# A conformer's depthwise convolution: one of eight feature tiles moves from TensorE to GpSimd

## The reference, cut to what matters

```python
def conformer_conv_mixer(x, w_pw1, b_pw1, w_dw, b_dw, ln_g, ln_b, w_pw2, b_pw2):
    h = x @ w_pw1 + b_pw1
    a, gate = jnp.split(h, 2, axis=-1)
    h = a * jax.nn.sigmoid(gate)
    h = causal_depthwise_conv(h, w_dw) + b_dw          # 31 taps, each feature by itself
    hf = h.astype(F32)
    mean = jnp.mean(hf, axis=-1, keepdims=True)
    var = jnp.mean(jnp.square(hf - mean), axis=-1, keepdims=True)
    hf = (hf - mean) * lax.rsqrt(var + LN_EPS) * ln_g.astype(F32) + ln_b.astype(F32)
    h = jax.nn.silu(hf).astype(x.dtype)
    return h @ w_pw2 + b_pw2
```

## Time and profile before

| what | value |
|---|---|
| median of the runs | 1980.66 us |
| the profiled execution's own time | 1981.02 us |
| its span in the profile | 1979.2 us |
| PE busy | 1964.8 us (99%) |
| DVE busy | 1342.4 us (68%) |
| ACT busy | 965.2 us (49%) |
| POOL busy | 46.2 us (2%), 89 instructions |

### The profile page before, as it was taken

The page is one execution under the profiler, slowest core; times in us unless marked ns, Lnnn a source line. Parts: engine busy times, 40 slices in busy tenths (PEclk is TensorE's granted clock), DMA queues, the critical chain, the costliest instruction groups (busy, mean ns, idle before and its releaser), DMA issues.

```text
span 1979.2 us, 26437 instructions
## 1 busy us (share of the span) xinstructions
PE 1964.8 (99%) x11074; PEld 1676.9 (85%) x11074; DVE 1342.4 (68%) x1496; ACT 965.2 (49%) x1148; POOL 46.2 (2%) x89
## 2 busy tenths in 40 slices
PE   9999999999999999999999999999999999999998
PEld 7889888888988887788888688889888888778887
DVE  5876666687566775676568866666865667667565
ACT  6655444655544543354445554454544444345443
POOL 0000000000000000000000000000000000000000
PEclk9999999999999999999999999999999999999999
DMA  8425654523665555546657455547565555455653
GB/s 256 131 86 172 205 190 158 172 97 124 220 202 187 190 172 190 171 146 195 209 194 207 130 197 189 191 154 234 192 202 191 172 195 187 159 173 170 200 191 107
DMA packets 239559, 351.70 MB, mean 178 GB/s; under 512 B 15952, under 2 KB 134096, under 8 KB 239440
## 3 DMA queue, kind: packets, MB, share of 16 engines
q1 hardware_dynamic: 238320, 348.22, 54.0%
q10 hardware_dynamic: 1120, 1.78, 0.3%
HBM read 344.83 MB, written 1.05 MB: 175 GB/s over the span
## 4 chain that ended last, share of the span: by engine, by line
PE 96%; DVE 2%; ACT 1%; DMA 1%; issue 1%; SPq 0%; DVEq 0%; ACTq 0%
PE psD L2205 19%; PE psD L2223 15%; PE psD L2224 15%; PE psD L2228 13%; PE psD L2214 9%; PE psD L2188 3%; PE psD L2187 3%; PE psD L2192 3%; PE psD L2226 2%; PE psD L2563 1%; PE psD L2511 1%; PE psD L2635 1%; PE psD L2636 1%; PE psD L2879 1%; PE psD L2307 1%; PE psD L2264 1%
## 5 line engine op out<-in xcount | busy, mean ns | idle before, releaser
L1217 DVE TENSOR_TENSOR wl<-raw,wh 128x2048 fp32r<-128x2048 f32 (+2 forms) x327 | 723.4, 2219 | 258.0 <-ACT wh L671 257.5
L671 ACT ACTIVATE wh<-raw 128x2048 fp32r<-128x2048 f32 (+2 forms) x327 | 605.3, 1855 | 303.2 <-PE psD L2226 243.0
L2205 PE MATMUL psD<-AHL,wh 128*128 128x512 f32 x1664 | 396.0, 390 | 0.0
L2205 PEld LDWEIGHTS psD<-AHL,wh 128*128 128x128 f32 x1664 | 307.8, 188 | 60.9
L2223 PE MATMUL psD<-wh,HH 128*128 128x512 f32 x864 | 339.1, 392 | 0.1
L2224 PE MATMUL psD<-wl,HH 128*128 128x512 f32 x864 | 336.6, 390 | 0.0
L2228 PE MATMUL psD<-wh,HL 128*128 128x512 f32 x735 | 286.1, 389 | 0.0
L2214 PEld LDWEIGHTS psD<-AHL,wl 128*128 128x128 f32 x1560 | 200.9, 191 | 8.1
L2214 PE MATMUL psD<-AHL,wl 128*128 128x256 f32 x1560 | 203.4, 283 | 0.0
L2223 PE MATMUL psD<-wh,AHL 128*128 128x512 f32 (+3 forms) x504 | 194.5, 386 | 1.7 <-DVE AHL L1253 1.7
L2223 PEld LDWEIGHTS psD<-wh,HH 128*128 128x128 f32 x864 | 162.4, 188 | 33.4 <-DVE wl L1217 0.5
(11 more groups left out here) (407 smaller groups left out, 2277.5 us busy)
## 6 DMA issues: line engine op xcount, KB each, us to landing
raw<-in_mlp_w SPq DMA_DIRECT2D x128, 1024.0 KB, 5.4
raw<-in_ret_w_in SPq DMA_DIRECT2D x48, 1024.0 KB, 5.2
raw<-in_w_gate SPq DMA_DIRECT2D x20, 1024.0 KB, 5.4
raw<-in_w_up SPq DMA_DIRECT2D x20, 1024.0 KB, 5.3
raw<-in_w_down SPq DMA_DIRECT2D x20, 1024.0 KB, 5.6
raw<-in_ret_w_out SPq DMA_DIRECT2D x16, 1024.0 KB, 5.0
raw<-in_w_in SPq DMA_DIRECT2D x15, 1024.0 KB, 5.5
raw<-in_cf_w_pw SPq DMA_DIRECT2D x12, 1024.0 KB, 6.1
```

Source lines behind the costliest of these rows:

```text
L671: e.activation(wh[q % NHL][:, 0:kt * n], raw[q % NRAW][:, 0:kt * n], ACT.Copy).then_inc(*up("act_wh", q))
L1217: e.tensor_tensor(wl[q % NHL][:, 0:kt * n], raw[q % NRAW][:, 0:kt * n], wh[q % NHL][:, 0:kt * n].bitcast(F32), ALU.subtract).then_inc(*up( ...
L2205: e.matmul(psD[pair][:, f, :], hi[:, k, fs], both[:, k, :, :], start=k == 0, stop=False, skip_group_check=True)
```

## The change

Feature 3 leaves PE's list: `CONV` has six entries. GpSimd takes it in 62 instructions. It waits for `hp` 3, then makes for each of the 31 taps a product (a tensor_scalar), and adds it to one of two partial sums (a tensor_tensor), even and odd taps apart; the first product of each starts its sum. One addition joins the two in `HC` feature 3 (after PE's first feature, whose tap weights lay there), and one multiplication makes its square. The four buffers of this are `PT3`, whose place is free because PE's copies of features 0 to 3 shrink to 0 to 2. Every addition waits for its product, every product for the addition before last.

DVE builds one set of tap weights less, does `taps` in steps to 14, 22, 28 and 31 in place of 8, 18, 26 and 31, and adds GpSimd's feature and square last (`pool_sums`), in place of the fifth `sums`. PE waits for these two additions before it sums `SM` and `SS`. The tap weights and PSUM banks of the features behind feature 3 move up by one place, and so features 4, 5 and 6 are PE's fourth, fifth and sixth.

```diff
-CONV = (0, 1, 2, 3, 4, 5, 6)
-TAPS = {"a": (0, 4), "b": (4, 2), "c": (6, 1)}
-CBANK = (0, 1, 2, 3, 6, 7, 0)
+CONV = (0, 1, 2, 4, 5, 6)
+TAPS = {"a": (0, 3), "b": (4, 2), "c": (6, 1)}
+CBANK = (0, 1, 2, 3, 6, 7)
...
@@ sync_program: the DMAs of XA
-                    e.wait_ge(*at("dve_cf", "hp", 3))
+                    e.wait_ge(*at("dve_cf", "hp", 2))
...
@@ gpsimd_program
+                    e.wait_ge(*at("dve_cf", "hp", 3))
+                    for k in range(31):
+                        w, x = VEC[:, V_DW + 93 + k:V_DW + 94 + k], HP[:, 3, k:S + k]
+                        o, m = PT3[:, k % 2, :], PT3[:, 2 + k % 2, :]
+                        if k == 0:
+                            e.tensor_scalar(o, x, w, VEC[:, V_BD + 3:V_BD + 4], ALU.mult, ALU.add).then_inc(*up("pool_cf", "tap", k))
+                        elif k == 1:
+                            e.tensor_scalar(o, x, w, None, ALU.mult).then_inc(*up("pool_cf", "tap", k))
+                        else:
+                            e.wait_ge(*at("pool_cf", "tap", k - 2))
+                            e.tensor_scalar(m, x, w, None, ALU.mult).then_inc(*up("pool_cf", "product", k))
+                            e.wait_ge(*at("pool_cf", "product", k))
+                            e.tensor_tensor(o, o, m, ALU.add).then_inc(*up("pool_cf", "tap", k))
+                    e.wait_ge(*at("pe_cf", "whole", 0))
+                    e.wait_ge(*at("pool_cf", "tap", 30))
+                    e.tensor_tensor(HC[:, 3, :], PT3[:, 0, :], PT3[:, 1, :], ALU.add).then_inc(*up("pool_cf", "whole"))
+                    e.wait_ge(*at("pool_cf", "whole"))
+                    e.tensor_tensor(PT3[:, 0, :], HC[:, 3, :], HC[:, 3, :], ALU.mult).then_inc(*up("pool_cf", "square"))
...
@@ vector_program, conformer
+                def pool_sums(n):
+
+                    e.wait_ge(*at("pool_cf", "whole"))
+                    e.wait_ge(*at("dve_cf", "sm", n))
+                    e.tensor_tensor(SM, SM, HC[:, 3, :], ALU.add).then_inc(*up("dve_cf", "sm", "pool"))
+                    e.wait_ge(*at("pool_cf", "square"))
+                    e.wait_ge(*at("dve_cf", "ss", n))
+                    e.tensor_tensor(SS, SS, PT3[:, 0, :], ALU.add).then_inc(*up("dve_cf", "ss", "pool"))
...
-                taps(8)
+                taps(14)
                 low_to(c + 1)
                 tap_squares(5)
-                tap_squares(6)
-                taps(18)
+                taps(22)
                 sums(1)
-                taps(26)
+                taps(28)
                 sums(2)
                 sums(3)
                 taps(31)
...
                 sums(4)
-                sums(5)
+                pool_sums(4)
...
@@ tensor_program, conformer
-                e.wait_ge(*at("dve_cf", "sm", last - 1))
+                e.wait_ge(*at("dve_cf", "sm", "pool"))
...
-                e.wait_ge(*at("dve_cf", "ss", last - 1))
+                e.wait_ge(*at("dve_cf", "ss", "pool"))
```

More of the change, by code:

```diff
@@ L319, in build @@
         HC, MN = carve(2 * DM, (8, S), (S,))
-        HP, XA, XC, SM, SS, B2W, WT0 = carve(5424, (8, S + 31), (4, 4 * (S + 31)), (4, S + 31), (S,), (S,), (DM,), (1024,))
+        HP, XA, XC, SM, SS, B2W, WT0, PT3 = carve(5424, (8, S + 31), (4, 3 * (S + 31)), (4, S + 31), (S,), (S,), (DM,), (1024,), (4, S))
         YS, = carve(5424, (8, S))
@@ L323, in build @@
         XB = AHL[:, :, :].rearrange("p a b -> p (a b)")[:, 0:8 * (S + 31)].bitcast(F32).rearrange("p (b m) -> p b m", b=4)
-        WT = (AR[:, 2 * DM:2 * DM + 1024], WT0, XS[:, 0, :], XS[:, 1, :], AR[:, 4400:5424], WT0, XS[:, 0, :])
-        WT_BEFORE = {5: 1, 6: 2}
+        WT = (AR[:, 2 * DM:2 * DM + 1024], WT0, XS[:, 0, :], XS[:, 1, :], AR[:, 4400:5424], WT0)
+        WT_BEFORE = {5: 1}
         U, CV = carve(2 * DM, (8, S + 2), (8, S))
@@ L1951, in sums @@
                         e.wait_ge(*at("dve_cf", "sm", n - 1))
-                    e.tensor_tensor(SM, SM if n > 1 else HC[:, 0, :], HC[:, n, :], ALU.add).then_inc(*up("dve_cf", "sm", n))
+                    e.tensor_tensor(SM, SM if n > 1 else HC[:, CONV[0], :], HC[:, CONV[n], :], ALU.add).then_inc(*up("dve_cf", "sm", n))
                     e.wait_ge(*at("act_cf", "sq", n))
@@ L2899, in conformer @@
                 for n, f in enumerate(CONV):
-                    x = "a" if n < 4 else "b" if n < 6 else "c"
+                    x = "a" if f < 4 else "b" if f < 6 else "c"
                     tile, at_ = {"a": XA, "b": XB, "c": XC}[x], (f - TAPS[x][0]) * (S + 31)
                     e.wait_ge(*at("dve_tap", n))
-                    if n == 0:
+                    if f == 0:
                         e.wait_ge(*at("dma_xa", 3, 3))
-                    elif n == 4:
+                    elif f == 4:
                         e.wait_ge(*at("dma_xb0", 1, 3))
                         e.wait_ge(*at("dma_xb1", 3, 3))
+                    elif f == 5:
                         e.wait_ge(*at("dve_cf", "aa", 1))
-                    elif n == 6:
+                    elif f == 6:
                         e.wait_ge(*at("dma_xc0", 2, 3))
                         e.wait_ge(*at("dma_xc1", 3, 3))
-                        e.wait_ge(*at("act_cf", "sq", 0))
                     for g in range(8):
```

## The result

The changed kernel takes 2008.28 us (median of four runs, 2007.38 to 2008.51) against 1980.68 (four runs of the kernel before); the ratio is 1.0136 with an interval of 1.0124 to 1.0148. It is 27.6 us slower. Forecast were 8.7 us more, with a range up to 1999. The direction was right and the size off by a factor of three.

What follows compares the result with a forecast made beforehand. DVE was taken to bound the end of the convolution stage, with PE less than a microsecond ahead. -3.8 + 9.9 + 2.6 = 8.7 us on 1980.7 gave 1989.4 us, range 1977 to 1999.

Steps and rivals of the forecast that it cites:

- GpSimd's own time: Feature 3 on GpSimd: pairs of 1.10 us (product 0.40, addition 0.62), 34 us in all, ending at 1108 if alone.
- PE one feature less, DVE's new order: Convolution stage: PE 3.48 us less, DVE's last addition at 1112.03 in place of 1115.81; gain 3.8 us.
- The DMAs of `XB`: Copies into `XB` land just before PE's fourth feature reads it at 1100.0; cost 0, at most 0.5 us.
- The highest bound: GpSimd's additions at three streams and products at two: 2002.5 us for the kernel.
- the sign of being too low: GpSimd's instructions: the forecast is too low if a product takes 0.6 us or an addition over 0.8.
- GpSimd held by DVE: GpSimd's instructions alternate with DVE's and wait behind weight chunks, so GpSimd is through at 1118 instead of 1108.
- DVE held by GpSimd: GpSimd's SBUF reads delay DVE's two-input instructions by 9.9 us; PE's sum of `SM` at 1122.0, 6.1 us later.
- its signs: On DVE: taps 0.5 to 0.65 us apart in place of 0.40, weight chunks 0.3 to 0.4 us longer.
- The first rival: DVE and GpSimd don't hold each other for whole instructions; the 3.8 us gain stands, 1976.9 us; chance 0.15.
- the second: Rival: only GpSimd waits and DVE is never held; 1985.5 us; chance 0.15.
- Half the clock at the sums: After PE's 9 to 10 us rest, six pairs of sums run at half clock, 5.2 us for 2.6: 2.6 more.
- The third rival: GpSimd slow by itself, a pair of 1.4 to 1.5 us, and holding small; 1984.5 us; chance 0.08.

Runs made afterwards that it cites:

- e2: The changed kernel with each of GpSimd's 62 instructions replaced by a memset of the same output, feature 3 left as zeros; 1977.21 us, ratio 0.9981.
- e7: The changed kernel with GpSimd's 29 pairs on 128 of the 256 tokens, half of feature 3 mostly left out; 1993.17 us, one run.
- e1: The kernel before with 62 GpSimd instructions added, 31 pairs of product and addition on constants, waited for by nobody; 1992.91 us, ratio 1.0060.
- e3: The changed kernel with 15 of feature 3's 31 taps on GpSimd, the other 16 left out of the result; 1986.39 us, ratio 1.0024.
- e6: The changed kernel with GpSimd's 29 products as tensor_tensor, the weight spread by a stride of zero, same result; 2001.20 us, ratio 1.0103.

## Why the prediction was wrong

The step that failed is "GpSimd's own time": 34 us were predicted for 62 instructions, and they take 53. With it went the path. The prediction had DVE as what is waited for and GpSimd through ahead of it; in the changed kernel DVE waits 18.94 us for GpSimd. The other steps held in kind, one of them in size partly by luck.

- **PE one feature less, DVE's new order: -3.8.** Right. e2 measured 3.7, and its last addition ends 0.12 us after the predicted moment.
- **The DMAs of `XB`: 0.** Right: PE's fourth feature starts at 1099.96 without a wait in the profile after.
- **GpSimd's own time: 34 us, end 1108 by itself.** Wrong: 52.1 us until feature 3 is ready, 53 with its square. Two first products, 29 pairs of 1.70 and the last addition are 1.85 + 49.4 + 0.8. The step built an addition as 0.19 us and two streams of 0.84 ns, and a product as 0.19 and one, from a memset. The addition is 2.1 ns an element (0.72 in place of 0.62); the product 2.5 (0.92 in place of 0.40). Most of the error is the product, 0.52 us x 29 = 15.1: a memset, which reads nothing, was the nearest row by its width and not by its work. The highest bound had two streams for a product, 0.62, and three for an addition, 0.83, a pair of 1.53 against 1.70; it gave 2002.5, and the range stopped below it, at 1999. The measured time is above both. The prediction had named the sign of being too low, "if a product takes 0.6 us", and it came. The Trainium skill's figure for an fp32 addition ("GPSIMD Engine Reference", Performance versus the Vector engine: 4497 ns for 2048 elements, 2.2 ns each) agrees with e7's 2.1; weighing it in would have mended the addition, not the product.
- **GpSimd held by DVE.** Predicted were 10 us (1118 less 1108), measured 66.5 less 52.1, 14.4. Four products beside weight chunks make 9.4 of them: 3.86, 3.04, 2.96 and 3.21 less 0.92 each. Its own length was off by 19 us and this by 4.4; together they move its end, the square included, from 1118 to 1141.2, behind DVE.
- **DVE held by GpSimd: PE's sum at 1122.0.** Right as a mechanism (e1, e3 against e2), but not on the path. DVE ended its own work at 1121.40, 9.6 us behind e2, against 9.9 predicted. That the size fits is in part luck: the 9.9 were built for all 62 instructions, and only 39 had started when DVE was through; with the 2.0 us swallowed by the rest ahead of 1090.31, that is 11.6 us over 39 instructions where the prediction had 11.9 over 62. Nor did all its signs come: three of the four weight chunks kept their 2.28 to 2.29 us and one took 2.83, where 0.3 to 0.4 more were expected of each. The prediction took this as the term that decides; in the changed kernel it is hidden under GpSimd's 18.94 us more. The first rival (nobody holds anybody) and the second (only GpSimd waits) both fall with e1.
- **Half the clock at the sums: +2.6.** Right in kind, 1.8 in size. The prediction counted six pairs; feature 7's is done before `SM` arrives and costs nothing, and the last ran mostly at the full clock again (L2960 takes 0.69 for two, the others 1.06).
- **The third rival**, GpSimd slow by itself and the holding small, had a chance of 0.08 and is half of what happened. GpSimd was slow by itself, but its pair of 1.45 us was too short, and the holding isn't small: 14.4 us on GpSimd, and 9.6 on DVE. It gave 1984.5, where 1.70 and the holding gave 2008. The case that both are true at once had no chance of its own.

The sum as it should have been, put together from the profile after: PE's sum of `SM` at 1073.8 + 52.1 + 14.4 = 1140.3, and 0.5 to PE, 1140.8; 24.96 later than before, and 1.8 for the clock: 26.8.

Not tried: GpSimd's additions on products made by ACT, which rests for nearly two thirds of the stage. By e1 and e6 I would expect its reads to hold DVE still; no run shows it.

## What to carry to other kernels

Before work is moved to an engine that stands still, measure one of its instructions in the exact form, with the widths and operands it will have; a row of another operation on the same engine gives the fixed part (0.19 us here) and not the price of an element. Then lay its length against the moment it is waited for: 62 instructions of 0.72 to 0.92 us can't fit in 37. And GpSimd, though idle, was not a free engine here, where VectorE works on two inputs in SBUF: the two took turns, and both got slower. Ask also whether two rivals can be true at once, and give that case its price.

## What the runs showed of the hardware

- GpSimd's multiplication of one fp32 tile by a weight for each partition (0.92 us for 256 elements) takes longer than the addition of two tiles (0.72); with a constant in place of the weight it takes 0.85, and written as a product of two tensors with a stride of zero, 0.61 where nothing held it.
- Turns between the engines depend on GpSimd's inputs: beside products with one input tensor and additions in alternation DVE's taps come every 0.63 us (three in a pair of 1.89), beside instructions with two input tensors every 0.81 (one for each). A memset of the same size holds nothing: beside memsets four instructions of tap weights took 1.42 us, as without, and 2.16 beside GpSimd's products and additions.
- A GpSimd product that meets a weight chunk of 2.29 us on DVE takes 2.0 to 2.3 us longer than alone, and 2.9 where it starts with the chunk and tap weights follow.
